# Six input panels of block 2 computed with the high and low activations as one 512-column moving operand

## The reference, cut to what matters

```python
h = h + 0.5 * swiglu(rms_norm_2(h, ffn1_norm[l]), ffn1_w_gate[l], ffn1_w_up[l], ffn1_w_down[l])
u = rms_norm_2(h, mix_norm[l])
z = u @ w_in[l]
qa, ka, va, qb, kb, vb, ga, gb = jnp.split(z, SPLITS, axis=-1)
...
ya = neighbourhood_attention_2d(qa, ka, va, na_rpb[l])
qb = rope(qb.reshape(B, T, NB_HEADS, HEAD_DIM), pos)
kb = rope(kb.reshape(B, T, NB_KV_HEADS, HEAD_DIM), pos)
...
yb = windowed_gqa_sink(qb, kb, vb, sink_logit[l])
merged = jax.nn.sigmoid(ga) * (ya @ w_branch_a[l]) + jax.nn.sigmoid(gb) * (yb @ w_branch_b[l])
h = h + merged @ w_out[l]
```

## Time and profile before

| | |
|---|---|
| median of 3 runs | 968.14 us (968.08 to 969.96) |
| profiled execution, its time | 968.35 us |
| profiled execution, its span | 966.5 us |
| granted TensorE clock over the span | 0.998 of full |
| TensorE matmul busy | 949.6 us, 5454 instructions |
| TensorE weight load busy | 832.6 us |
| VectorE busy | 653.5 us |
| ScalarE busy | 531.6 us |
| HBM | 178 GB/s over the span |

### The profile page before, as it was taken

The page is one execution under the profiler, slowest core; times in us unless marked ns, Lnnn a source line. Parts: engine busy times, 40 slices in busy tenths (PEclk is TensorE's granted clock), DMA queues, the critical chain, the costliest instruction groups (busy, mean ns, idle before and its releaser), DMA issues.

```text
span 966.5 us, 14023 instructions
## 1 busy us (share of the span) xinstructions
PE 949.6 (98%) x5454; PEld 832.6 (86%) x5454; DVE 653.5 (68%) x833; ACT 531.6 (55%) x689; POOL 59.8 (6%) x94
## 2 busy tenths in 40 slices
PE   6999999999999999999999999999999999999997
PEld 6999988888888888888888888999888898888886
DVE  5787688865755556687666666878656576566664
ACT  6676678635544444474544445679664464444543
POOL 4000000000100000022321000100000020000000
PEclk9999999999999999999999999999999999999999
DMA  9665343554756565537675655545334546665541
GB/s 289 212 220 173 100 163 107 202 192 153 239 176 197 191 192 198 174 131 240 204 236 190 217 174 174 169 141 170 131 131 160 188 168 202 192 198 179 189 155 43
DMA packets 117405, 173.11 MB, mean 179 GB/s; under 512 B 3120, under 2 KB 89408, under 8 KB 117360
## 3 DMA queue, kind: packets, MB, share of 16 engines
q1 hardware_dynamic: 115824, 168.32, 53.6%
q0 software_dynamic: 1392, 3.91, 1.3%
q10 hardware_dynamic: 144, 0.26, 0.1%
HBM read 171.43 MB, written 1.05 MB: 178 GB/s over the span
## 4 chain that ended last, share of the span: by engine, by line
PE 54%; DVE 0%; issue 0%; POOLq 0%; ACT 0%; POOL 0%; DVEq 0%
PE pair L663 15%; PE pair L666 8%; PE acc L633 5%; PE acc L634 5%; PE acc L635 5%; PE pair L633 4%; PE pair L635 4%; PE pair L634 4%; PE acc L1121 1%; PE acc L1107 1%; PE acc L1098 0%; PE acc L1099 0%; PE pair L726 0%; PE pair L731 0%; PE acc L731 0%; PE acc L727 0%
## 5 line engine op out<-in xcount | busy, mean ns | idle before, releaser
L663 PE MATMUL pair<-actp,wh 128*128 128x512 f32 x912 | 293.1, 396 | 0.4 <-DVE arena L1967 0.2
L1627 DVE TENSOR_TENSOR wl<-raw,wh 128x2048 fp32r<-128x2048 f32 x89 | 204.5, 2297 | 68.0 <-ACT wh L1224 68.0
L1224 ACT ACTIVATE wh<-raw 128x2048 fp32r<-128x2048 f32 x88 | 168.4, 1913 | 85.0 <-PE acc L635 85.0
L666 PEld LDWEIGHTS pair<-actp,wl 128*128 128x128 f32 x912 | 171.3, 188 | 39.9
L666 PE MATMUL pair<-actp,wl 128*128 128x256 f32 x912 | 179.2, 278 | 0.0
L1218 ACT ACTIVATE wh<-raw 128x2048 fp32r<-128x2048 f32 x69 | 132.1, 1916 | 79.8 <-PE pair L635 55.1
L1622 DVE TENSOR_TENSOR wl<-raw,wh 128x2048 fp32r<-128x2048 f32 x68 | 155.4, 2287 | 25.1 <-ACT wh L1218 24.8
L663 PEld LDWEIGHTS pair<-actp,wh 128*128 128x128 f32 x912 | 141.8, 189 | 2.4 <-issue 0.4
L1424 ACT ACTIVATE arena<-pair 128x512 f32<-128x512 f32 x57 | 34.2, 599 | 173.4 <-PE pair L663 173.4
L633 PE MATMUL acc<-wh,midh 128*128 128x512 f32 x312 | 121.8, 390 | 0.1
L635 PE MATMUL acc<-wh,midl 128*128 128x512 f32 x312 | 121.4, 389 | 0.0
(11 more groups left out here) (307 smaller groups left out, 1361.9 us busy)
## 6 DMA issues: line engine op xcount, KB each, us to landing
raw<-in_w_in SPq DMA_DIRECT2D x37, 1024.0 KB, 5.2
raw<-in_mlp_w SPq DMA_DIRECT2D x32, 1024.0 KB, 5.4
raw<-in_ffn_w_gate SPq DMA_DIRECT2D x22, 1024.0 KB, 5.3
raw<-in_ffn_w_up SPq DMA_DIRECT2D x22, 1024.0 KB, 5.3
raw<-in_ffn_w_down SPq DMA_DIRECT2D x22, 1024.0 KB, 4.8
raw<-in_w_out SPq DMA_DIRECT2D x8, 1024.0 KB, 4.9
raw<-in_w_up_rnn SPq DMA_DIRECT2D x4, 1024.0 KB, 5.4
raw<-in_cmp_k_w SPq DMA_DIRECT2D x2, 1024.0 KB, 5.4
```

Of the source, the lines that this page charges most:

```text
L663: return nc.tensor.matmul(bank[:, :].rearrange("p (u t) -> p u t", u=2), h[:, k, cs], actp[:, :, k, :], **kw)
L666: return nc.tensor.matmul(bank[:, 0:T], l[:, k, cs], acth[:, k, :], **kw)
L1224: nc.scalar.activation(wh[:, n % R, :], raw[:, n % R, :], ACT.Copy).then_inc(hi_ready, 1)
L1627: nc.vector.tensor_tensor(wl[:, n % R, :], raw[:, n % R, :], wh[:, n % R, :].bitcast(F32), ALU.subtract).then_inc(lo_ready, 1)
```

## The change

Panels +1, +4, +5, +6, +7 and +8 go from `feature_tile` to `halved_tile`. Each takes a pair of banks (banks 0 and 1, or 6 and 7 for +5 and +7) where it took one. ScalarE copies the right halves of both tiles into a new tile `qk` as the first thing of its turn behind the panel, ahead of the key copies and of `hi(n + 2)`, after waiting until the evacuation before has read `qk`. VectorE waits for that copy, adds the left halves, waits for its own sum, and evacuates from `qk` where it evacuated from PSUM. The waits of TensorE for free banks are set to the new pairs. Panel +0 stays as it was.

```diff
--- before.py
+++ after.py
@@ -339,6 +339,8 @@
         ff_hi = sem("ff_hi")
         ff_lo = sem("ff_lo")
 
+        qk_right = sem("qk_right")
+        qk_sum = sem("qk_sum")
         qa_evac = sem("qa_evac")
         ka_evac = sem("ka_evac")
         va_evac = sem("va_evac")
@@ -610,6 +612,11 @@
         GATE_BANKS = (HIGH, LOW)
         UPA_BANKS = (LAST, HIGH)
         UPR_BANKS = (LOW, LAST)
+        HALVED2 = (KA2[0], QA2[1], KA2[1], KBVB, QB, QB + 1)
+        qk = carve(12544, 2, T)
+
+        PAIR2 = dict(zip(HALVED2, (pair01, pair01, pair67, pair01, pair67, pair01)))
+
         GATE2_BANKS = (LAST, LOW)
         BR_BANKS = (LAST, LOW)
         MRG_BANKS = ((HIGH, LOW), ((2, 3), LAST))
@@ -1135,8 +1142,8 @@
 
             def free_bank2(n):
 
-                last = {VA2: (qa_evac, 1), KA2[1]: (ka_evac, 1), KBVB: (qa_evac, 2), QB: (ka_evac, 2),
-                        QB + 1: (kv_evac, 1), GA2: (va_evac, 2), GA2 + 2: (qb_evac, 2), GB2: (ga_evac, 4 + 2),
+                last = {VA2: (qa_evac, 1), QA2[1]: (ka_evac, 1), KA2[1]: (va_evac, 2), KBVB: (qa_evac, 2), QB: (ka_evac, 2),
+                        QB + 1: (kv_evac, 1), GA2: (qb_evac, 1), GA2 + 2: (qb_evac, 2), GB2: (ga_evac, 4 + 2),
                         GB2 + 2: (ga_evac, 4 + 4)}
                 if n in last:
                     pe.wait_ge(*last[n])
@@ -1154,7 +1161,7 @@
                 free_bank2(n)
                 if n in col2:
                     for c in range(2):
-                        m = feature_tile(n, KT, c, ps[n % 2][:, c * T:(c + 1) * T], acth, actl)
+                        m = halved_tile(n, c, PAIR2[n][:, c, :])
                         if c == 1:
                             m.then_inc(panel_done, 1)
                         elif n == QKV2 + 1:
@@ -1543,6 +1550,13 @@
                     gates2(n)
                 if n in (BR + 3, WO2 + 1):
                     merge_hi(1, int(n == WO2 + 1))
+                if n - 1 in HALVED2:
+                    done(n - 1)
+                    if n - 1 != KA2[0]:
+
+                        act.wait_ge(*{QA2[1]: (ka_evac, 1), KA2[1]: (qa_evac, 2), KBVB: (ka_evac, 2), QB: (kv_evac, 1),
+                                      QB + 1: (qb_evac, 1)}[n - 1])
+                    right_half(qk, PAIR2[n - 1]).then_inc(qk_right, 1)
                 if n - 1 in KA2:
                     u = KA2.index(n - 1)
                     act.wait_ge(ka_evac, u + 1)
@@ -2117,9 +2131,14 @@
 
             for n in range(QKV2, F2):
 
-                bank = FIRST2 if n - 1 == QKV2 else two(ps[(n - 1) % 2][:, :])
+                bank = FIRST2 if n - 1 == QKV2 else qk
                 if n == QKV2 + 1:
                     take_scales(3)
+                if n - 1 in HALVED2:
+                    at = HALVED2.index(n - 1)
+                    dve.wait_ge(qk_right, at + 1)
+                    add_right(qk, PAIR2[n - 1]).then_inc(qk_sum, 1)
+                    dve.wait_ge(qk_sum, at + 1)
                 if n - 1 in (*QA2, QB, QB + 1):
                     done(n - 1)
                     dst, ev, u = ((qaT, qa_evac, QA2.index(n - 1)) if n - 1 < QB else (qbT, qb_evac, n - 1 - QB))
```

## The result

The changed kernel takes 969.41 us (median of 20 runs, 968.69 to 970.75); the kernel before, timed beside it, 968.11 us (20 runs). The ratio of the runs is 1.0018, with a 95% interval of 1.0011 to 1.0024: slower by about 1.75 us, between 1.1 and 2.3. The loss is clear of nought, and the interval lies on both sides of the 0.2% that the prediction drew as its line.

The account below looks back on a forecast made before the run. TensorE, busy 949.6 of 966.5 us, was taken as the bound. New waits of 3.07 us less 1.04 from the panels gave +2.03, so 970.2 us against the median; range 967.9 to 971.4, likeliest case 969.5 to 970.9.

Parts of the forecast that it names:

- The likeliest case: Whole kernel: panel gains less than new TensorE waits, +2.0 us to 970.2, range 969.5 to 970.9; chance 0.62.
- What bounds the kernel: Attention stage of block 2: TensorE never stops except at the first score, where it already waits 0.17 us.
- The panels' gain: Six halved panels: each 5.58 us instead of 5.75, 0.174 saved a panel, 1.04 us in all.
- slot 0: First score, behind panel +1's keys: the unhidden sum delays the evacuation, so TensorE shifts by +0.8 us.
- slot 4: Behind panel +5: the normalisation comes 1.87 us later, TensorE waits 0.75 for it; shift +1.03.
- slot 6: ScalarE's queue around panel +7: copy2 and exp2 about 2.5 us late, TensorE waits 0.25 and 0.30; shift +1.23.
- slot 7: Behind panel +8's right-half copy: copy2 and exp2 about 2.3 us late, TensorE waits 0.50 and 0.30; shift +2.03.
- (A): All six panels: added work hides behind slack everywhere, also at the first score, giving 967.1 us; chance 0.09.
- (B): Only the first score is late; later head slots find their work ready, about 968.1 us; chance 0.13.
- (C): Every new step brings two more hand-overs of 0.05 to 0.1 us, up to 971.4 us; chance 0.12.
- (D): Six panels: the wide matmul saves 0.04 instead of 0.17 us a panel, giving 971.0 us; chance 0.04.
- (E): Six panels: the wide operand runs slower here than in the feed-forward; left out, no chance given.

Follow-up runs that it names:

- e3: Changed kernel without the right-half copies and sums, all six panels still halved: stage 118.95 us, against 119.97 for the kernel before.
- e11: Changed kernel with only panels +7 and +8 halved, the other four as before: stage 120.81 us, against 119.97 for the kernel before.
- e4: Changed kernel with narrow matmuls as before, but a same-size copy and maximum behind each of six panels: stage 122.59 us, against 119.97 before.
- e2: Changed kernel with panel +1 as before, the other five halved: stage 121.08 us, against 119.97 for the kernel before.
- e8: Changed kernel with only panels +4 and +6 halved: stage 119.63 us, against 119.97 for the kernel before.
- e1: Changed kernel with only panel +1 halved, the other five as before: stage 120.81 us, against 119.97 for the kernel before.
- e6: Changed kernel with the right-half copy behind panel +4 made twice: stage 121.88 us, against 121.85 for the changed kernel.
- e9: Changed kernel, +1 and +5 unhalved, +7's swap on GpSimd, +8's behind ScalarE's exponentials: stage 119.21 us; kernel 967.34 us, ratio to before 0.9997.
- e10: Changed kernel with only panels +4 and +6 halved, run again and timed: stage 119.59 us; kernel 967.09 us, ratio to before 0.9998.
- e7: Changed kernel with the rotations' quarter swaps moved from ScalarE to GpSimd: stage 121.35 us, against 121.85 for the changed kernel.
- e12: The kernel before, unchanged, traced a second time: stage 119.98 us, against 119.97 in its first trace.

## Why the prediction was right

The point, 970.2 us for the median, was 0.8 us too high; as a difference it said +2.0 where +1.75 was timed and +1.88 read from the stage. The likeliest case had the right sign, the right price of each panel's gain, and the right mechanism at slots 0 and 4; at slots 6 and 7 it had the right engines but not the right path, and came out near the measured waits in part by luck. Its size was a little too large. That put more of the chance beyond the 0.2% line (0.54) than the measured 0.18% bears out.

**What bounds the kernel** held: the wait of 0.17 us at the first score was the one place where TensorE already waited for the chain in question, and it is where the first panel's gain turned into a loss.

**The panels' gain**, 1.04 by the sum, was 1.02 in e3. In after, panel +5 takes from 634.99 to 640.57:

```profile
634.99 0.40 PE L670 MATMUL pair<-actp,wh 128*128 128x512 f32 x1
...
640.57 0.33 PE L1128 MATMUL acc<-arena 128*128 128x64 f32 x2
```

5.58 us, the figure of the sum.

**The slots**, shift by shift, foretold and measured (where TensorE's first matmul of the slot starts, and for slots 6 and 7 after the slot's waits): slot 0 +0.8 and +0.82; slot 4 +1.03 and +0.98, with 0.08 more at the transposes behind it; slot 6 +1.23 and +1.07; slot 7 +2.03 and +1.90. The waits, 3.07 by the sum, were 0.99 + 0.78 + 0.32 + 0.78 = 2.87. Less 1.04 that is 1.83; the remaining 0.05 of the +1.88 stands at slot 7, where the score starts 0.41 us behind the awaited transposes and before 0.36.

**The term that was mis-sized** is slot 6: 0.55 by the sum, 0.32 measured. I gave TensorE 0.14 us from any engine's end, from one row where it had waited for VectorE. Behind VectorE it is 0.14 and 0.15 again (620.59 to 620.73, 648.45 to 648.60), behind ScalarE only 0.04 to 0.05. And the queue was 2.40 late ahead of `copy2` of slot 6, not 2.5. A part of that comes from the step that I put at 1.42 us: its parts as I listed them add up to 1.44, and of the three hand-overs one was there before. Behind +5 copy and sum took 1.36, from the copy's start at 640.76 to the evacuation's at 642.12. Together these took the wait ahead of slot 6's mix from 0.25 to 0.03, and slot 7's from 0.50 to 0.48.

**The path that was wrong** is that of slots 6 and 7. I had the lag of +5 and +6 "carried in the queues". e11 has waits of the same size (+1.18) without that lag: what sets slot 6 is the right-half copy of +7, which keeps the key copies back until panel +7 is done. In the whole change the carried lag ends within 0.05 us of it, so the sum came out near the measured one either way. For slot 7 I had `hi` behind the right-half copy of +8 at +2.3 and the rest following. `hi` is late by only 1.94 (from 55.12 to 57.06 behind the start of panel +1), since ScalarE goes on from that copy after 0.48 us and not 0.60 (664.56 to 665.04), and starts it before the exponentials' last readout has ended. The swaps then wait 0.30 for VectorE's evacuation of +8, which my account of slot 7 left out, and `copy2` is late by 2.22; without that wait the mix would have waited about 0.18 and not 0.48 (an estimate from these rows). Too much for ScalarE's queue and nothing for VectorE's nearly cancelled: that is the luck in the 0.50 for 0.48.

**The signs** that the prediction named were there (the matmuls, 5.58 us a panel, the later score, 0.7 us at slot 4, `hi` behind +8 more than 1 us after its panel) but for one: of the four waits of 0.2 to 0.5 at slots 6 and 7 the first was 0.03.

**The rivals.** (A), the gain alone, falls: e4 has the cost without the gain. (B), only the first score, falls by e2 and e11, where slots 4 and 7 wait without it. (C), deeper by more hand-overs, points the wrong way: hand-overs were shorter. (D), no gain of the wide matmul here, falls by e3, and so does (E), a wide operand that runs slower here: the panels of e3 take 5.57 us. The claim that free-bank waits and later loads cost nothing agrees with e3 and e8, which have all the pairs of banks and no new wait. At slot 8 ScalarE still has 1.02 us to spare, of 2.26:

```profile
679.88 1.92 ACT L1225 ACTIVATE wh<-raw 128x2048 fp32r<-128x2048 f32 x1 [1.02 <-PE pair L642]
```

## What to carry to other kernels

A form that was good in one loop brings its follow-up work along. Before it is moved to another place, the slack between the end of each tile and its first consumer has to be read there, tile by tile: the same copy and sum were free behind two panels, and brought waits of 0.8 and 1 us behind two others and of 1.2 us behind the last two together. The place in the queue counts too: a step that must wait for a panel's end, put ahead of one that need not, holds both. Where a bound engine waits for in-order queues of other engines, carry each queue forward from the rows of before plus a shift, and at each hand-over between them take the later one; here that foretold nine stage lengths (e1 to e6, e8, e9, e11) to within 0.2 us. And a change worth a thousandth is read from the length of its own stage in the trace, not from timed medians.

## What the runs showed of the hardware that was not expected

**The start of the kernel has two lengths.** The first matmul of panel +1 stood between 607.90 and 610.19 us in the 14 traces, with the same work ahead. e8 and e10 are the same kernel, instruction for instruction. TensorE's first matmuls of 256 columns, in e8 and in e10:

```profile
13.45 0.28 PE L654 MATMUL pair<-actp,wl 128*128 128x256 f32 x1
...
15.13 0.28 PE L654 MATMUL pair<-actp,wl 128*128 128x256 f32 x1
```

```profile
12.74 0.41 PE L654 MATMUL pair<-actp,wl 128*128 128x256 f32 x1
...
15.72 0.40 PE L654 MATMUL pair<-actp,wl 128*128 128x256 f32 x1
```

Between the two rows lie 14 steps in both. In e8 they take 0.12 us each, as elsewhere in the kernel at the full 2.4 GHz; in e10 they take 0.213 us, which is 256 columns at 1.2 GHz. The granted clock of this stretch reads 1.00 in both. TensorE had stood idle up to 8.6 and 7.7 us, and had had four groups of transposes and 1 us of idle time since. So it belongs to the single execution and not to the kernel. Six traces have the slow start (before, e2, e7, e9, e10, e12) and eight the fast one. Seven of the eight fast ones reach panel +1 between 607.90 and 608.05 (e8, whose first matmul itself came 0.9 us late, at 608.81), and five of the six slow ones between 609.09 and 609.50 (e7, late in the same way, at 610.19). What decides between the two was not tried. The difference explains why two single executions could not be subtracted here: before had the slow start and after the fast one, so 968.82 - 968.35 is 0.47 us, and 1.5 us of difference at the start hides the rest. It is also what the two groups of times look like, though only the profiled executions show their start.

**Equal copies on GpSimd are not equally long.** Four copies of 32 x 512 with a wait between them took 2.62 us once and 4.91 us once, four of 32 x 256 took 3.70 (e7); in e9 four of 32 x 512 took 4.74. The lengths are those of the rows; for two of the four the VectorE instruction that reads the result starts 0.03 to 0.04 us behind the row's end (658.14 and 658.17 in e7, 663.18 and 663.22 in e9). ScalarE takes 2.56 and 1.70 for the same, each time.

**The hand-over to TensorE depends on who releases it**: 0.14 to 0.15 us from VectorE, 0.04 to 0.05 from ScalarE, in the rows above, counted from the end of the releaser's row. Why was not tried.
